# Sparse attention: six of the eight products of projected keys placed among the index scores of query blocks 2 to 5

## The reference, cut to what matters

```python
proj = h @ w_in                       # -> q_lat 256, c_kv 128, k_idx 64, w_idx 8
q     = q_lat @ w_uq                  # 16 heads of 64
q_idx = q_lat @ w_qi                  # 8 index heads of 64
# per block of 128 queries:
rel   = relu(einsum('bqhd,bsd->bqhs', q_idx, k_idx))
score = einsum('bqh,bqhs->bqs', w_idx, rel)        # -inf where not admissible
_, idx = top_k(score, 256)                         # 256 keys for each query
logits = einsum('bqhc,bqkc->bqhk', q_abs, c_kv[idx]) - slope * dist
p = softmax(logits);  o_lat = p @ c_kv[idx]
```

## Time and profile before

| what | us |
|---|---|
| median of 3 runs | 3289.56 |
| those runs | 3284.58, 3289.94, 3289.56 |
| profiled execution, its time | 3282.8 |
| profiled execution, its span | 3281.0 |
| first pair of index scores | 172.7 |
| first key product | 206.6 |
| first look of the search | 209.4 |
| step 0, first reduction | 269.2 |

### The profile page before, as it was taken

How to read it: one execution, slowest core, us unless ns; L and a number is a source line. 1 busy time by engine, 2 the same in 40 slices (tenths; PEclk the granted TensorE clock), 3 DMA queues, 4 the chain that set the end, 5 groups by cost and what they waited for, 6 DMA issues and landing times.

```text
span 3281.0 us, 62708 instructions
## 1 busy us (share of the span) xinstructions
PE 2989.3 (91%) x25842; PEld 2376.8 (72%) x25842; DVE 1682.3 (51%) x2306; ACT 1060.5 (32%) x1594; POOL 1458.6 (44%) x1457
## 2 busy tenths in 40 slices
PE   5889788889999999998999799999778999999997
PEld 5734466677777887776678578888767878777886
DVE  4477987565454454557033255665534434443446
ACT  2267566312211212115332255455212212111212
POOL 1101000235566655666355345565144555565553
PEclk6799999999999999998999899999889999999998
DMA  5300000442232222321533311211031111111111
GB/s 203 116 13 14 1 1 1 155 128 61 74 92 81 66 72 74 95 62 42 192 114 92 109 49 49 88 56 53 27 109 33 52 47 40 42 51 58 40 42 72
DMA packets 230039, 226.84 MB, mean 69 GB/s; under 512 B 16430, under 2 KB 198273, under 8 KB 229825
## 3 DMA queue, kind: packets, MB, share of 16 engines
q1 hardware_dynamic: 216368, 177.27, 17.6%
q10 hardware_dynamic: 13457, 46.45, 3.9%
HBM read 185.67 MB, written 37.75 MB: 68 GB/s over the span
## 4 chain that ended last, share of the span: by engine, by line
PE 45%; issue 17%; POOL 17%; DVE 10%; DMA 5%; ACT 2%; POOLq 1%; DVEq 0%; SPq 0%; ACTq 0%; PEldq 0%; PEld 0%
POOL w_hi L149 9%; POOL w_lo L151 8%; PE ps L139 8%; PE ps L141 8%; PE ps L140 8%; DMA w_raw<-in_f_w_up_dram 2%; PE ps L2531 2%; DMA w_raw<-in_f_w_down_dram 2%; PE ps L2543 2%; DVE d_junk L1396 2%; PE ps L1162 2%; PE ps L1185 1%; PE ps L1174 1%; PE ps L2456 1%; PE ps L2580 1%
## 5 line engine op out<-in xcount | busy, mean ns | idle before, releaser
L149 POOL TENSOR_TENSOR w_hi<-w_raw,ones 128x128 fp32r<-128x128 f32 (+1 forms) x568 | 473.0, 833 | 1134.0 <-PE ps L141 970.3
L749 DVE SCALAR_TENSOR_TENSOR uc<-u,pc,uc 128x1024 f32<-128x1024 f32 x176 | 272.8, 1551 | 600.8 <-ACT uc L733 588.6
L139 PE MATMUL ps<-hn_hi,w_hi 128*128 128x512 f32 x1408 | 553.0, 393 | 26.6 <-POOL w_lo L151 18.5
L151 POOL TENSOR_TENSOR w_lo<-w_raw,w_hi 128x128 fp32r<-128x128 f32 (+1 forms) x568 | 557.2, 981 | 44.5
L140 PE MATMUL ps<-hn_lo,w_hi 128*128 128x512 f32 x1408 | 550.0, 391 | 0.0
L141 PE MATMUL ps<-hn_hi,w_lo 128*128 128x512 f32 x1408 | 549.8, 390 | 0.0
L732 ACT ACTIVATE u<-ps 128x1024 f32<-128x1024 f32 x88 | 90.4, 1028 | 938.5 <-PE ps L141 933.8
L139 PEld LDWEIGHTS ps<-hn_hi,w_hi 128*128 128x128 f32 x1408 | 265.7, 189 | 90.4 <-issue 17.6
L141 PEld LDWEIGHTS ps<-hn_hi,w_lo 128*128 128x128 f32 x1408 | 265.6, 189 | 55.6
L140 PEld LDWEIGHTS ps<-hn_lo,w_hi 128*128 128x128 f32 x1408 | 265.8, 189 | 54.5
L139 PE MATMUL ps<-g_hi,w_hi 128*128 128x512 f32 x704 | 279.8, 397 | 10.6 <-POOL w_lo L151 9.7
(11 more groups left out here) (368 smaller groups left out, 5533.9 us busy)
## 6 DMA issues: line engine op xcount, KB each, us to landing
w_raw<-in_f_w_up_dram SPq DMA_DIRECT2D x88, 512.0 KB, 3.9
f_ada_w<-in_ada_w_dram SPq DMA_DIRECT2D x48, 512.0 KB, 4.0
rwkv_scratch<-rp_stage ACTq DMA_DIRECT2D x48, 512.0 KB, 3.0
w_raw<-in_f_w_down_dram SPq DMA_DIRECT2D x176, 128.0 KB, 2.2
rc_raw<-rwkv_scratch SPq DMA_DIRECT2D x32, 512.0 KB, 3.9
d_r<-in_ada_w_dram ACTq DMA_DIRECT2D x24, 512.0 KB, 6.1
ada_w<-in_ada_w_dram SPq DMA_DIRECT2D x16, 512.0 KB, 8.6
xin<-in_x_dram SPq DMA_DIRECT2D x8, 512.0 KB, 7.4
```

What stands on the lines that cost most here:

```text
L139: pe.matmul(out, w_hi, x_hi, start=first, stop=False)
L149: pool.tensor_tensor(hi, raw, one, ALU.mult).then_inc(k.w_hi_done, 1)
L151: pool.tensor_tensor(k.w_lo[s][:, tiles, :], raw, hi.bitcast(F32), ALU.subtract).then_inc(k.w_split if n else k.w_half, 1)
L749: dve.scalar_tensor_tensor(out=c[wi][:, :], in0=u[wi][:, tap:tap + S], scalar=k.pc[:, bass.ds(i * (2 * FF_TILES) + col, 1)], in1=c[wi][:, ...
```

## The change

Six of the eight key products (`AHEAD = len(U1)` = 6) leave the projection loop. One is written after each piece of `U1` in TensorE's list (`key_pe`), so one behind every fourth pair. Their copies (`key_act`) are written into ScalarE's list of relus: five of them after the second relu of pieces 2 to 6, the sixth after the last relu. The projection loops begin at 6. The places of the signs are counted from `AHEAD`. `EARLY` goes from 19 to 17, so two rounds more stand in the loop. The masks of blocks 2 to 5 are made at steps 15, 15, 16, 17, where it was 13, 14, 15, 16, and within a step ahead of the search of the next blocks and the look of the round, where they stood behind it.

```diff
@@ -1221,6 +1221,24 @@
                              start=j == 0, stop=j == IDX_HEADS - 1)
         last.then_inc(sem["y_ps"], 1)
 
+    AHEAD = len(U1)
+
+    def key_pe(pe, o):
+        out = k.ps[2 + o % 2]
+        if o == 0:
+            pe.wait_ge(sem["w_landed"], 16 * 4)
+        if o >= 2:
+            pe.wait_ge(sem["pre_sb"], o - 1)
+        for c in range(NH):
+            cols = slice(c * HALF, (c + 1) * HALF)
+            last = pe.matmul(out[:, cols], w_uk[:, 2 * o:2 * o + 2, :].rearrange("p h d -> p (h d)"), ckv_t[:, cols],
+                             start=True, stop=True)
+        last.then_inc(sem["pre_ps"], 1)
+
+    def key_act(act, o):
+        act.wait_ge(sem["pre_ps"], o + 1)
+        act.activation(k_t[:, o, :], k.ps[2 + o % 2][:, :], ACT.Copy).then_inc(sem["pre_sb"], 1)
+
     def pe_attention(pe):
         for m in range(4):
             for t in range(2):
@@ -1240,10 +1258,10 @@
                                      start=True, stop=True)
                 last.then_inc(sem["x1_ps"], 1)
                 n += 1
-        for o in range(3 * PAIRS):
+                if n % 4 == 0:
+                    key_pe(pe, n // 4 - 1)
+        for o in range(AHEAD, 3 * PAIRS):
             m, out = o % PAIRS, k.ps[2 + o % 2]
-            if o == 0:
-                pe.wait_ge(sem["w_landed"], 16 * 4)
             if o >= 2:
                 pe.wait_ge(sem["pre_sb"], o - 1)
             for c in range(NH):
@@ -1321,7 +1339,10 @@
                 act.activation(rel1[e][:, 0:c1 - c0], bank(2 * (n % 2) + e)[:, 0:c1 - c0], ACT.Relu
                                ).then_inc(sem["relu1"], 1)
                 r += 1
-        for o in range(3 * PAIRS):
+                if r % 8 == 2 and r > 8:
+                    key_act(act, r // 8 - 1)
+        key_act(act, AHEAD - 1)
+        for o in range(AHEAD, 3 * PAIRS):
             m, src = o % PAIRS, k.ps[2 + o % 2]
             act.wait_ge(sem["pre_ps"], o + 1)
             if o == PAIRS:
@@ -1335,7 +1356,7 @@
                     act.wait_ge(sem["scale"], A_HEADS)
                 act.activation(o_t[:, m, :], src[:, :], ACT.Copy, scale=q_scale[:, m:m + 1]).then_inc(sem["pre_sb"], 1)
             for i in range(EARLY):
-                if min(4 * i // 3 + 1, 3 * PAIRS - 1) == o:
+                if min(AHEAD + 4 * i // 3 + 1, 3 * PAIRS - 1) == o:
                     sign_act(act, 0, i)
         for m in range(4):
             act.wait_ge(sem["qi_ps"], 8)
@@ -1463,7 +1484,7 @@
         dve.scalar_tensor_tensor(out=d, in0=equal[:, 0:n], scalar=UNSELECTED, in1=edge_of(s),
                                  op0=ALU.mult, op1=ALU.add).then_inc(sem["masked"], 1)
 
-    EARLY = 19
+    EARLY = 17
     SECOND, ALONE, LAST = 2 * PAIRS + 1, 2 * PAIRS + 1 + COMMON, 6 * PAIRS
 
     def round_with(A):
@@ -1483,7 +1504,7 @@
         return 2, range(0)
 
     def masked_in(A):
-        return {13: (2,), 14: (3,), 15: (4,), 16: (5,), LAST - 2: (6,), LAST + 6: (7,)}.get(A, ())
+        return {BITS - EARLY: (2, 3), 16: (4,), 17: (5,), LAST - 2: (6,), LAST + 6: (7,)}.get(A, ())
 
     def dve_attention(dve):
         dve.wait_ge(sem["edge"], 1)
@@ -1540,6 +1561,8 @@
                                          ALU.add, ALU.min, small[:, 0, h:h + 1]).then_inc(sem["x_min"], 1)
             if A % 4 == 0 and A:
                 sums_dve(A // 4 - 1)
+            for m in masked_in(A):
+                search_end(dve, m)
             if A == SECOND:
                 search_begin(dve, 1)
             if round_with(A) is not None:
@@ -1548,8 +1571,6 @@
             for r in alone:
                 look(dve, i, r)
                 settle(dve, i, r)
-            for m in masked_in(A):
-                search_end(dve, m)
         sums_dve(GROUPS - 1)
         scale_out(GROUPS - 1)
```

## The result

| | before | after |
|---|---|---|
| median of 6 runs, us | 3285.28 | 3298.99 |
| those runs | 3282.06 to 3289.94 | 3297.3 to 3300.53 |
| profiled execution: time, span | 3282.8, 3281.0 | 3300.53, 3298.8 |

The ratio is 1.004, with a 95% interval from 1.0027 to 1.0053, which is 8.9 to 17.4 us: slower, as forecast (+10.95 us). The two profiled executions lie 17.7 us apart.

The account below looks back on a forecast made before the run. Index scores were taken to run at VectorE's pace, projections at TensorE's, last search rounds at late signs'. 4.1 − 8.6 + 7.7 + 7.75 = +10.95 us gave 3300.5, own range 3297 to 3304.5, 8 in 10 from 3286 to 3307.

Parts of the forecast that it names:

- index scores: Index scores of blocks 2 to 5 end 4.1 us later: copies 3.2, products 1.4, clock −0.5.
- products taken off: Five key products leave the projection stretch, at 1.72 us each: 8.6 us less.
- five signs instead of two: Behind the last query copy, three more signs each wait for a 2.58 us VectorE round: +7.7 us before step 0.
- so step 0: Start of the attention loop: 4.1 − 8.6 + 7.7 makes it 3.2 us later.
- rounds and masks in the loop: From step 13, two more rounds run at TensorE's pace, then all masks follow without cover: +7.75 us.
- second search: First look of the second search, 354.32 us before, comes about 11 us later, the whole sum of +10.95.
- Copies: Index scores: inserted key copies delay ScalarE's relus, 0.59 us each in 512-wide pieces, together 3.2 us.
- Products: Index scores: inserted key products delay TensorE's next pairs, 1.0 us behind the thin piece, 0.4 behind the first, together 1.4.
- The clock: Index scores, thin 128-wide piece: clock fall likely to come again there; taken as −0.5 us, bounds −1.3 to +3.4.
- rival B: Products set step 0 but the loop pays: −4.5 + 7.75 = +3.2 us, 3292.8; chance 0.18.
- A: TensorE sets the pace before step 0 and at steps 15 to 17, search covered: −4.5 us, 3285.1; chance 0.14.
- C: Clock fall in the index scores lasts across two inserted products: total +14.85 us, 3304.4; chance 0.14.

Follow-up runs that it names:

- e8: Kernel before plus five extra key-sized copies among the relus, products where they were; one run, first look 2.5 us behind before.
- e7: Changed kernel with all six key copies put after the last relu, some keys wrong; one run, first look 1.2 us behind before.
- e3: Kernel before with only the six key products and copies moved and signs counted from AHEAD, still 19 rounds ahead; ratio 1.0042.
- e1: Changed kernel with only the signs of block 5 placed nearer their rounds, none behind the last copy; ratio 1.0018.
- e12: e10 repeated unaltered, on one chip with e11; ratio 0.9985 to the kernel before, median 3282.05 us.
- e2: Kernel before with only 17 rounds ahead instead of 19 and the masks at steps 15, 15, 16, 17; ratio 1.0032.
- e4: e3 with the nearer sign places of e1: keys moved, 19 rounds ahead, masks where they were; ratio 0.9997.
- e5: Kernel before with nearer signs, 21 rounds ahead instead of 19 and masks at steps 11 to 14; ratio 0.9992.
- e10: Kernel before with e5's signs, 21 rounds ahead and the masks cut into instructions spread over steps 11 to 16; ratio 0.9971.
- e11: e10 with the six key products and copies moved among the index scores and e1's signs; ratio 0.998, median 3283.69 us.
- e6: Kernel before with nearer signs, 22 rounds ahead and whole masks at steps 10 to 13; ratio 1.0025.
- e9: Kernel before with e5's signs, 22 rounds ahead and the masks cut into instructions spread over steps 10 to 16; ratio 0.999.

## Why the prediction was right

Each term at its landmark, in us:

| term | predicted | measured |
|---|---|---|
| index scores | +4.1 | +3.5 |
| products taken off | −8.6 | −9.6 |
| five signs instead of two | +7.7 | +7.9 |
| so step 0 | +3.2 | +1.9 |
| rounds and masks in the loop | +7.75 | +8.15 |
| second search | +10.95 | +9.8 |

Measured are: 40.27 − 36.76; (85.18 − 91.25) − 3.51; 13.20 − 5.26 for the time from the last query copy to step 0; and 36.41 − 28.26 from step 13 to the second search.

*Index scores.* The sum came out near, with its parts shifted, and that they made up for each other is luck. Copies 2.5 (e8) for 3.2, the 512-wide one 0.55 for 0.59. Products about 2.3 (e7) for 1.4: behind the thin piece VectorE waited 1.68 where 1.0 was reckoned, behind the first 0.87 where it was 0.4. The clock gave back about 1.1 for 0.5; this and the 2.3 rest on one estimate. That ScalarE's strict order is what makes the copies dear is shown by e8, which has no product there.

*Products.* The last query copy moved by 1.0 us more than five products alone. The prediction took the stretch to run at TensorE's pace, but there TensorE also waits for ScalarE: before, the eight key products took 14.20 us for 8 × 1.72 = 13.76 (206.58 to 220.78), and among the values it waited 0.59 and 0.60 us for copies; after, it waited 0.59 once. Copies and signs share ScalarE, and which of them holds it up was not tried.

*Signs.* The cost of a late sign held: five give 13.20 us, seven 18.36 (e3), 2.58 apart, so rival B is out. The start of the sum was read wrongly: the 5.26 us are TensorE's index queries with their copies, as e1 and e12 have them with no sign behind the last copy. That 5.26 + 3 × 2.58 came out is luck, for in before the second sign ended together with those products. Had it ended earlier, the third would have been free in part. Of the 7.94 us, 7.73 are three spacings of signs (263.23 to 270.96); the first logits at half clock account for the rest.

*Loop.* The step held in size and in kind; e2 alone shows it without keys. The covered time of steps 13 and 14 is what was given up.

*Rivals.* A is out at both of its places: TensorE waited 8.94 us before step 0 and 4.62 and 11.09 us while the masks were made. It needed less than 2.0 us in the index scores; it was 3.5. C did not come in this execution. In e1 and e4 the fall came with one product in it, and cost 1.66 us at the first look; it never met two. Some executions with the products in have it and some not, on the same list of instructions up to there.

*What the prediction had not.* The granted clock of the first steps of the loop. In the stretch from 3 to 8 us after step 0 it was 1.00 in before, after, e2, e5, e10 and e12, and steps 0 to 12 took 56.37 to 56.88 us; it was 0.50 to 0.66 in e1, e3, e4, e7, e8 and e11, and they took 58.03 to 59.90. (It was 1.00 in e6 and e9 too, but they make masks in these steps.) TensorE's code is the same. In e8, the first row here, and in before, the second, TensorE had been idle for 1.30 us ahead of step 0:

```profile
277.51:282.51 5.00, 4.33 (x8) 1.61 (x9) 2.77 (x13) 4.03 (x12) 0.00 (x0) 0.53 0.00 2
```

```profile
272.18:277.18 5.00, 4.32 (x19) 1.82 (x19) 3.26 (x18) 4.17 (x14) 0.00 (x0) 1.00 0.00 2
```

The changed kernel lost nothing there (56.67 us), so its forecast held; in e1, e3, e4 and e11 it goes with 1.1 to 3.3 us of what was measured, and most of the 4.4 us between e11 and e12. That the clock costs this time is read from its going along with it, in six executions against six; no experiment set the clock. What decides on it was not found: idle time of 2.96 us and more ahead of step 0 (after, e3, e4, e7, e11) always gave a start at half clock, but in after that clock had ended 3 us later.

*The rest.* 13.7 us is the difference of the medians, 9.8 that at the second search. Of the 17.8 us between the two spans, 2.9 came before the first pair and 0.5 between the second search and the end of the attention (612.4 and 625.6 us), and 4.6 after it, in layers whose code is the same. No experiment aimed at these; the runs of after itself spread over 3.2 us. The forecast of +10.95 lies within the interval of 8.9 to 17.4. It took none of this remainder into account, and why the later layers took longer stays open. The time that was forecast, 3300.5, is near the measured 3298.99 by luck in part: it was counted from a median before of 3289.56, which is 3285.28 with all six runs, and the loss was 2.8 us larger than forecast.

## What to carry to other kernels

Work moved into an engine's idle time still has to be taken away by another engine, and where that engine works strictly in order, each copy delays what stands behind it: ask what is next in the evacuating engine's line, not only where TensorE idles. When a stage is shortened on one engine, find what else runs beside it; here the search beside the projections needed their length, and rounds pushed into the loop took covered time from the masks. The gain lay elsewhere: more of the search ahead, and VectorE's long masks cut into pieces that fit under TensorE's steps, which e10 and e12 show at 0.9971 and 0.9985.

## What the runs showed of the hardware

- The granted clock is not a function of the instruction list. The products of index queries, same code, ran at 1.00 before (7.13 us) and began at 0.50 after (9.94 us). At the thin piece it fell to 0.50 in all eight kernels that have no product there (before, e2, e5, e6, e8, e9, e10, e12); with products in, it stayed up in after, e3, e7 and e11 and fell in e1 and e4. The Trainium skill ("TensorE: Matmul & The Clock Gate", Part 1) says that the throttled state is the default and activity releases it. The direction agrees. The same part calls the effect "run-variable", and the two outcomes for one list of instructions, after and e1 at the thin piece, agree with that too.
- Two of VectorE's instructions on 128x384 tiles took 1.51 and 1.44 us beside GpSimd's (e6, and the same in e9), and 0.56 alone, while GpSimd's went from 1.27 to 1.80. Which resource they share, no run here separates.
- In these runs TensorE came back from longer idle time at half clock: after 2.28 us, ahead of the sums of step 16 in before, these took 1.98 us for 1.09 in e10; after 3.67 us its next products took 2.08 us for 1.13 (e6), and after 2.96 to 14.10 us ahead of step 0 the first logits took 0.80 us for 0.49 (e4, e11, e7, after, e3). With 1.30 us of idle time they took 0.49 in the other nine, and in e1 and e8 the clock fell all the same within the next 8 us.
